# A streaming-encoder layer on one core: who stores the operands of the first pair, in what order its loads, splits and sums stand, and where the fourth row tile lives

## The reference

```
h    = rmsnorm(x) * norm_g                       # 1024 x 2048
proj = h @ w_in                                  # 2048 x 5120, cut into nine parts
       A: u, v, gate (512 each)   spatial gating: u * (W_s @ layernorm(gelu(v)) + b_s)
       B: q (1024), k, v (256 each), gate (1024)   sliding-window attention with sinks and a bias
       C: input, gate (512 each)  trailing means over 2, 4, 8, 16 positions, a linear map, a scale
mix  = concat(A, B, C), each times silu(its gate)
x    = x + mix @ w_out                           # 2048 x 2048
out  = rmsnorm(x) * final_g
```

## Time and profile before

| what | value |
|---|---|
| median of 3 runs (lowest, highest) | 1207.43 us (1206.47, 1209.11) |
| the profiled execution: its time, its span | 1209.07 us, 1207.3 us |
| TensorE / VectorE / ScalarE busy, share of the span | 97% / 72% / 41% |
| mean TensorE clock granted | 0.991 of full |
| DMA moved | 361.27 MB, 299 GB/s |

### The profile page before, as it was taken

How to read it: one execution, slowest core, us unless ns; L and a number is a source line. 1 busy time by engine, 2 the same in 40 slices (tenths; PEclk the granted TensorE clock), 3 DMA queues, 4 the chain that set the end, 5 groups by cost and what they waited for, 6 DMA issues and landing times.

```text
span 1207.3 us, 15660 instructions
## 1 busy us (share of the span) xinstructions
PE 1176.0 (97%) x5862; PEld 956.6 (79%) x5862; DVE 872.0 (72%) x1150; ACT 493.4 (41%) x867; POOL 39.7 (3%) x80
## 2 busy tenths in 40 slices
PE   9989899999999999999999999999999999999995
PEld 7768788888888888888888877778877788888884
DVE  5589857586976776788677797988788366564675
ACT  5465564523544333355433362423344213323135
POOL 0012110000000000000000000000000000000000
PEclk9999899999999999999999999999999999999998
DMA  9989899877865565995566586699999689956878
GB/s 341 412 326 361 348 422 369 249 270 247 340 236 181 201 229 213 326 374 192 196 238 254 210 322 253 239 325 364 419 411 408 256 309 401 376 212 233 297 278 330
DMA packets 105772, 361.27 MB, mean 299 GB/s; under 512 B 10945, under 2 KB 18145, under 8 KB 94817
## 3 DMA queue, kind: packets, MB, share of 16 engines
q1 hardware_dynamic: 99936, 339.30, 76.1%
q0 software_dynamic: 5760, 20.97, 4.3%
HBM read 288.67 MB, written 71.57 MB: 298 GB/s over the span
## 4 chain that ended last, share of the span: by engine, by line
PE 74%; DVE 12%; DMA 8%; SPq 2%; issue 2%; ACT 1%; ACTq 0%; DVEq 0%
PE n_bank L1800 23%; PE n_bank L1802 22%; PE n_bank L1801 22%; DMA x_parts<-s_ring 3%; DVE w_lo L1255 2%; PE e_bank L1951 2%; DVE w_b L1380 2%; PE t_bank L1979 2%; PE t_bank L1962 1%; DMA w_b<-w_b_dram 1%; DMA m_parts<-tg 1%; DMA m_parts<-stage 1%; DVE s_ring L1264 1%; DMA rows<-x_dram 1%; SPq L529 1%
## 5 line engine op out<-in xcount | busy, mean ns | idle before, releaser
L924 ACT ACTIVATE w_hi<-w_b 128x1024 fp32r<-128x1024 f32 (+1 forms) x200 | 197.4, 1033 | 435.7 <-PE n_bank L1802 387.2
L1800 PE MATMUL n_bank<-s_ring,w_hi 128*128 128x512 f32 x896 | 356.8, 398 | 0.0
L1802 PE MATMUL n_bank<-s_ring,w_lo 128*128 128x512 f32 x896 | 349.0, 390 | 0.0
L1801 PE MATMUL n_bank<-s_ring,w_hi 128*128 128x512 f32 x896 | 348.9, 389 | 0.0
L1255 DVE TENSOR_TENSOR w_lo<-w_b,w_hi 128x1024 fp32r<-128x1024 f32 (+1 forms) x200 | 231.6, 1198 | 113.6 <-ACT w_hi L924 113.3
L1800 PE MATMUL n_bank<-w_hi,s_ring 128*128 128x512 f32 x672 | 266.2, 396 | 16.0 <-DVE w_lo L1255 5.8
L1801 PE MATMUL n_bank<-w_lo,s_ring 128*128 128x512 f32 x672 | 263.8, 393 | 0.0
L1802 PE MATMUL n_bank<-w_hi,s_ring 128*128 128x512 f32 x672 | 263.8, 392 | 0.0
L1800 PEld LDWEIGHTS n_bank<-s_ring,w_hi 128*128 128x128 f32 x896 | 168.1, 188 | 39.3 <-issue 2.2
L1802 PEld LDWEIGHTS n_bank<-s_ring,w_lo 128*128 128x128 f32 x896 | 168.2, 188 | 35.7
L1801 PEld LDWEIGHTS n_bank<-s_ring,w_hi 128*128 128x128 f32 x896 | 168.3, 188 | 35.3 <-issue 1.9
(11 more groups left out here) (211 smaller groups left out, 949.1 us busy)
## 6 DMA issues: line engine op xcount, KB each, us to landing
s_ring<-x_parts SPq DMA_DIRECT2D x224, 512.0 KB, 6.0
w_b<-w_b_dram SPq DMA_DIRECT2D x74, 1024.0 KB, 10.6
s_ring<-m_parts SPq DMA_DIRECT2D x112, 512.0 KB, 6.2
x_parts<-s_ring POOLq DMA_DIRECT2D x40, 512.0 KB, 10.2
m_parts<-stage SPq DMA_DIRECT2D x18, 512.0 KB, 8.3
x_parts<-s_ring SPq DMA_DIRECT2D x16, 512.0 KB, 15.1
rows<-x_dram SPq DMA_DIRECT2D x8, 1024.0 KB, 12.3
residual<-x_dram SPq DMA_DIRECT2D x6, 1024.0 KB, 9.2
```

The source lines that it names most:

```text
L924: sc.activation(w_hi[:, J % 2, part], w_source(J)[:, part], ACT.Copy).then_inc(hi_done, 1)
L1800: pe.matmul(psum_out, stat[0], mov[0], start=first, stop=False)
L1801: pe.matmul(psum_out, stat[0], mov[1], start=False, stop=False)
L1802: return pe.matmul(psum_out, stat[1], mov[0], start=False, stop=last)
```

## The change

It has these parts:

1. SyncE stores the operand tiles of periods 0 and 1 alone, GpSimd those of 2 to 13 (SAVED_EARLY 4 to 2). At n = 2 and n = 3 SyncE now waits until the four stores of that period have landed (`saves_done`), ahead of the a22 quads.
2. At the start each a11 tile is loaded ahead of the weight piece of its number, and in step 1 the operand is split ahead of the weights.
3. A11 + A12: the banks of A12 aren't copied by ScalarE any more; VectorE adds them straight to A11 in `add_chain` (in its steps 3 and 4), and `sum_y11` in step 6 is gone. `bank_free` of step 4 waits for that add.
4. In steps 3 and 4 the splits of weights and operands of the next step alternate differently on ScalarE and VectorE: first operand tile, weights, other operand tiles.
5. Row tile 3 has home 1 and is loaded at n = 9 (before: home 0, n = 8), tile 4 home 2 at n = 10 (before home 1, n = 9), tiles 5 and 6 homes 3 and 4, tile 7 home 3 again. The first add of S1 waits for three squared tiles, not four. The squares stand at the end of ScalarE's step; root, row factors and layer constants of the first half are one step later.

```diff
@@ -86,7 +86,7 @@
-ADDS = ({Q_A11: 0, Q_A12: 0, Q_S3: 0, Q_S2: 1, Q_S1: 2, Q_S4: 1, Q_A22: 1},) + tuple(
+ADDS = ({Q_A11: 0, Q_A12: 1, Q_S3: 0, Q_S2: 1, Q_S1: 2, Q_S4: 1, Q_A22: 1},) + tuple(
     {Q_A12: 1 if p >= PAIR_O or not early(p) else 0, Q_A11: 1 if early(p) else 0, Q_S2: 1, Q_S1: 2,
@@ -101,7 +101,7 @@
 def first_copies(p, st):
-    return ST * sum(1 for b in range(p) if early(b) and b < PAIR_O) + st + 1
+    return ST * sum(1 for b in range(PAIR_TA, p) if early(b) and b < PAIR_O) + st + 1
@@ -136,9 +136,9 @@
 ROW_TILES = HALVES * ST
-ROWS_LOADED = {5: 0, 6: 1, 7: 2, 8: 3, 9: 4, 11: 5, 13: 6, 15: 7}
-AT_ROOT = (10, 17)
-AT_ROWS = (12, 19)
+ROWS_LOADED = {5: 0, 6: 1, 7: 2, 9: 3, 10: 4, 11: 5, 13: 6, 15: 7}
+AT_ROOT = (11, 17)
+AT_ROWS = (13, 19)
 AT_KV = (13, 18)
@@ -146,7 +146,15 @@
 AT_SGU = ((17, 18), (20, 21))
-SAVED_EARLY = 4
+SAVED_EARLY = 2
+
+ROW_HOME = (0, 0, 0, 1, 2, 3, 4, 3)
+
+
+def row_loads(t):
+
+    return sum(1 for i in ROW_HOME[:t + 1] if i == ROW_HOME[t])
+
@@ -322,7 +330,7 @@
         row_buffers = [place(f"rows{i}", [P, D], offset=home) for i, home in enumerate(row_homes)]
-        row_tile = [row_buffers[max(t - ST + 1, 0)] for t in range(ROW_TILES)]
+        row_tile = [row_buffers[i] for i in ROW_HOME]
         kv = (y11[PAIR_F], y21[PAIR_F])
@@ -460,7 +468,7 @@
         w_loaded = [[sem(f"w_loaded{b}{c}") for c in range(2)] for b in range(3)]
-        w_summed, y11_summed, y21_summed = sem("w_summed"), sem("y11_summed"), sem("y21_summed")
+        w_summed, y21_summed = sem("w_summed"), sem("y21_summed")
         first_copied, p1_copied, u_copied = sem("first_copied"), sem("p1_copied"), sem("u_copied")
@@ -529,17 +537,24 @@
+            def saves_done(n):
+
+                for k in range(4):
+                    sp.wait_ge(f_saved_late[first_slot(n, k)[1]], 16 * ((n - SAVED_EARLY) // 2 + 1))
+
...
                     sp.wait_ge(f_lo_done, 20)
-                elif t < ST:
+                elif t < 3:
                     sp.wait_ge(rows_squared, t)
-                elif t < ST + 2:
+                elif t < 5:
                     sp.wait_ge(f_lo_done, 40)
+                elif t < 7:
+                    sp.wait_ge(s4_made, KB)
                 else:
-                    sp.wait_ge(s4_made, KB)
-                sp.dma_start(row_tile[t][:], x[P * t:P * t + P, :]).then_inc(rows_loaded[max(t - ST + 1, 0)], 16)
+                    sp.wait_ge(rows_squared, 6)
+                sp.dma_start(row_tile[t][:], x[P * t:P * t + P, :]).then_inc(rows_loaded[ROW_HOME[t]], 16)
@@ -551,7 +566,7 @@
             def load_layer_constants():
-                sp.wait_ge(rows_squared, 5)
+                sp.wait_ge(rows_squared, 4)
                 for dst, src in ((ln_g_sb[:], rows(ln_g, 512)), (ln_b_sb[:], rows(ln_b, 512)),
@@ -764,8 +779,8 @@
             for r in range(1, KB):
+                load_a11(r)
                 load_first(r // 4, r % 4)
-                load_a11(r)
             second, third = BUFS[0][1:]
@@ -778,6 +793,8 @@
                     save_early(n + 1)
+                if n in (2, 3):
+                    saves_done(n)
                 if n < 2:
@@ -790,7 +807,7 @@
                     save_table()
-                if n == 10:
+                if n == 11:
                     load_layer_constants()
@@ -962,7 +979,7 @@
-                sc.wait_ge(rows_loaded[max(t - ST + 1, 0)], 16 * (t + 1) if t < ST else 16)
+                sc.wait_ge(rows_loaded[ROW_HOME[t]], 16 * row_loads(t))
                 sc.activation(row_tile[t][:], row_tile[t][:], ACT.Square, accum_out=ssq_x[:, t:t + 1]
@@ -982,12 +999,12 @@
                 sc.wait_ge(f_lo_done, 4 * STEPS)
-                sc.wait_ge(rows_squared, ST + 2)
+                sc.wait_ge(rows_squared, 5)
                 if half == 1:
...
                     if half == 0:
-                        sc.wait_ge(y11_summed, st + 1)
+                        sc.wait_ge(y_added, added(PAIR_F, Q_A12, st))
                     else:
@@ -1113,7 +1130,7 @@
                     q = ORDERS[pp][jj // 2]
-                    if q == Q_A12 and early(pp) and pp < PAIR_O:
+                    if q == Q_A12 and early(pp) and PAIR_F < pp < PAIR_O:
                         copy_first(pp, sts)
@@ -1170,19 +1187,18 @@
                     for k in range(4):
+                        first_hi(1, k)
                         split_hi(1, (k,))
-                        first_hi(1, k)
                 elif J + 1 < TOTAL and J not in SUM_S3:
...
                 if 0 < J < STEPS - 1:
-                    for k in range(4):
+                    first_hi(J + 1, 0)
+                    if J in SUM_S3:
+                        split_hi(J + 1)
+                    for k in range(1, 4):
                         first_hi(J + 1, k)
-                if J in SUM_S3:
-                    split_hi(J + 1)
                 for r in SCALE_A22.get(J, ()):
                     scale_a22(r)
-                if J - 1 in ROWS_LOADED:
-                    square_rows(ROWS_LOADED[J - 1])
                 if J == AT_TABLE + 1:
@@ -1217,6 +1233,8 @@
                         job(kind, i)
+                if J - 1 in ROWS_LOADED:
+                    square_rows(ROWS_LOADED[J - 1])
                 if j == 2 * EARLY.index(Q_S2) + 1 and early(p) and p > PAIR_F:
@@ -1423,7 +1441,7 @@
                 if p == PAIR_F:
-                    ve.wait_ge(rows_squared, ST)
+                    ve.wait_ge(rows_squared, 3)
                 elif p == PAIR_TA:
@@ -1453,7 +1471,10 @@
                     wait_chain(ve, bank_done, group_done, n, st)
-                    if q == Q_A12:
+                    if q == Q_A12 and p == PAIR_F:
+                        ve.wait_ge(p1_copied, p1_copies(p, st))
+                        add(y11[p], st, y12[p])
+                    elif q == Q_A12:
                         if early(p):
@@ -1492,13 +1513,6 @@
-            def sum_y11(st):
-
-                ve.wait_ge(first_copied, first_copies(PAIR_F, st))
-                ve.wait_ge(p1_copied, p1_copies(PAIR_F, st))
-                ve.tensor_tensor(y11[PAIR_F][:, st, :], y11[PAIR_F][:, st, :], y12[PAIR_F][:, st, :], ALU.add
-                                 ).then_inc(y11_summed, 1)
-
@@ -1672,8 +1686,8 @@
                     for k in range(4):
+                        first_lo(1, k)
                         split_lo(1, (k,))
-                        first_lo(1, k)
                 if 0 < n < STEPS - 1:
@@ -1686,17 +1700,15 @@
                         first_lo(n + 1, 0)
+                        split_lo(J + 1, (0,))
                         first_lo(n + 1, 1)
-                        split_lo(J + 1)
+                        split_lo(J + 1, (1,))
                         first_lo(n + 1, 2)
...
                             first_lo(n + 1, k)
-                if n == 6:
-                    for st in range(ST):
-                        sum_y11(st)
                 if n == 8:
@@ -1834,7 +1846,7 @@
                 q = ORDERS[p][at]
-                if q == Q_A12 and early(p) and p < PAIR_O:
+                if q == Q_A12 and early(p) and PAIR_F < p < PAIR_O:
                     pe.wait_ge(first_copied, first_copies(p, st))
```

## The result

| | before | after |
|---|---|---|
| median of 7 runs (lowest to highest), us | 1207.43 (1206.47 to 1209.11) | 1211.76 (1209.50 to 1212.65) |
| profiled execution, its span | 1209.07, 1207.3 | 1211.76, 1210.0 |

The ratio after to before is 1.0030, 95% interval 1.0018 to 1.0042: slower by a little more than the 0.2% that can be told from no change. The range ended at 1210.7, so the result lies outside it, on the side of the second rival.

A forecast was written before the change was run, and what follows sets the result against it. TensorE, busy 97%, was the bound, so only its gaps could give time. 10.4 us lost at step 4 against gains at steps 5 and 10 left 2.1 us less: 1205.3 us median, range 1199 to 1210.7.

The forecast's parts named there:

- the second rival: Step 14: DMA backlog delays period 12's stores and the loads they release; 3.3 us more, 1210.7; chance 0.18.
- a third of the bytes: Before step 4: GpSimd's stores take a third of DMA bytes, SyncE's 7.34 MB take 26.5 us, B22's first half lands at 54.9.
- the first rival: Step 4: only period 2's stores pass B22, landing 50.8; step 4 starts at 59.8; 6.8 us less, 1200.6; chance 0.26.
- 9.0 us from B22's landing to step 4: Head of step 4: weight sum, splits, remaining tiles and the bank-freeing add take 9.0 us, so it starts at 64.5.
- The 4.54 us of its wait: Head of step 5: TensorE's wait, put down to SyncE's period 3 stores, goes: 4.54 us, plus 1.7 of clock.
- the sum: Steps 4 to 11: losses and gains added up to 2.1 us less, step 11 at 142.9, 1207.0 profiled, 1205.3 median.
- 10.4 us lost against some 6 won: Steps 4 and 5: 10.4 us lost at step 4; 4.54 of gap and 1.7 of clock won back at step 5.
- 6.5 forecast: Step 10: the wait for row tile 3 goes, worth 3.73 us between two steps and 2.75 of clock.
- its wait of 3.2 us: Step 14: the last load lands 2.4 us later while the need is 2.1 earlier, so TensorE waits 3.2.
- its 2.2 of clock: Step 14: the clock drop after the wait costs another 2.2 us.
- The third rival: Step 10: the first S1 add waits for VectorE's or the DMA's backlog; 4.4 us more, 1211.8; chance 0.04.
- a margin of 1.3 us at step 14's last load: Step 14: the last load landed at 179.3 before the change, 1.3 us ahead of TensorE's need.

The follow-up runs named there:

- e8b_stores_tiles: The kernel before with parts 1 and 5, without parts 2 to 4; 1208.53 us, ratio 1.0001.
- e1_stores_back: The changed kernel with part 1 undone: SyncE stores periods 0 to 3 again, without its two waits; 1204.37 us, ratio 0.9975.
- e13_back_later: e1_stores_back with row tile 5 loaded at n = 13 and tiles 5 to 7 behind the coming step's slot loads; 1199.93 us, ratio 0.9939.
- e2_tiles_only: The kernel before with part 5 alone; 1207.47 us, ratio 1.0006.
- e3: The changed kernel with row tiles 4 and 5 loaded and squared in their first 64 columns only, 2 MB less read; 1206.63 us, ratio 0.9997.
- e12: The changed kernel with row tile 5 loaded at n = 13 and tiles 5 to 7 behind the coming step's slot loads; 1207.59 us, ratio 1.0000.
- e14: e2_tiles_only with row tile 5 loaded at n = 13 and tiles 5 to 7 behind the coming step's slot loads; 1204.29 us, ratio 0.9981.

## Why the prediction was wrong

**Right, part 1.** B22's first half was to land at 55.5 and landed at 56.3; period 2's stores at 36 to 43 (measured 33.0 to 41.0), period 3's at 50 to 57 (47.3 to 56.3). The mechanism stands: undone, step 4 is back at 54.4. What I chose badly was the rate at which GpSimd's stores go past. I took a third of the bytes, from a stretch of 16 us. The DMA view of the changed kernel from 30 to 33 us, while its period 2 stores were under way (queue, packets, MB, share of the engines' time):

```profile
q1 hardware_dynamic: 192, 0.62, 51.2%
q0 software_dynamic: 169, 0.63, 51.0%
```

Half each, to the per cent (and 51.4 to 52.5 from 44.5 to 47.3). The third of the earlier trace rows was a mean over a stretch in which GpSimd's queue was empty part of the time. This is what the Trainium skill ("DMA: Bandwidth & Descriptors", section on queues, rings and completion order) says, turns between the queues that have work; the trace agrees. By it all eight stores are past B22, landing 55.9, 0.4 from what was measured, and the first rival, stores that slip past at less cost, had nothing left to stand on: 0.26 was too much for it. As a mean the third holds in the changed kernel too: from 28.0 to 56.3, the whole way of B22's first half, GpSimd's queue moved 4.19 of 11.60 MB, 36%, and all eight stores were past it all the same.

**Right, parts 3 and 4.** 9.0 us from B22's landing to step 4; measured 65.2 - 56.3 = 8.9. The wait ended on a VectorE add, as named. Not seen: that before's order, kept, would have needed only 5.0 us (issued 28.0, landed 27.7 later, step 4 at 60.7 in e8b_stores_tiles). So the late weight turned parts that win 4.4 us into ones that cost 3.8 at step 4.

**Right in number, wrong in cause, step 5.** The 4.54 us of its wait were won as forecast, but the sum gives part 1 the credit. With SyncE's stores back the wait is gone (e1_stores_back) or 0.74 us (e13_back_later): parts 2 to 4 do it alone, by the traces part 4. So part 1 was costed as a trade, 10.4 us lost against some 6 won, where beside the other parts it had next to nothing left to win. Step 3 lost 1.4 us to period 1's later stores, not 3, and that was hidden under step 4's wait as forecast.

**Right, part 5 up to step 11.** No wait at step 10; VectorE kept up; in e2_tiles_only it was worth 6.4 us there, against 6.5 forecast. Step 5 at 78.5 (forecast 77.6), step 11 at 143.8 (142.9): 0.9 late, of which 0.7 came in with step 4, no more than executions of the same code differ there. Between steps 11 and 14 0.4 of it was made up.

**The step that failed** was "From step 11 on I see nothing that changes by more than 0.2". In its place step 14 grew from 11.7 to 16.4 us: 4.7 us more. That is nearly all of the 4.8 us by which the profiled execution (1211.76) missed the 1207.0 that the sum gave for it. In the terms of the second rival: its wait of 3.2 us was 3.4; its 2.2 of clock wasn't paid in the changed kernel (1.00 from 148 to 190), though it was in e1_stores_back (0.92); another 1.3 of step 14 is spread over its starts. It gave 1210.7 for the median and so 1212.4 for the profiled execution; both were 1211.76. The third rival's 1211.8 is the measured number by chance: the wait at step 10 that it rests on didn't come.

So the case was on the list, with its sign (a wait of PE for s_ring at step 14), and had the wrong chance. What spoke for it were a DMA share of 1.02 on both sides of one idle stretch, and a margin of 1.3 us at step 14's last load. Two errors kept it at 0.18. First, I costed the later loads of tiles 3 and 4 at nothing because nothing waits for them. What counts is what is queued behind them: tile 4 moved to 141.5, and the constants from 140 to 147, into the one stretch that gave the DMA time to catch up. Every experiment with part 5's times of loading shows the longer step 14, with or without part 1 (e2 17.4, e8b 17.1, after 16.4 us), and most of it goes when the tiles' bytes go (e3, 12.1) or tile 5 goes behind (e12, e13, e14, 13.1 to 13.5). Second, I put its mechanism into the stores of period 12 alone. They do release the loads, as I had it, but they landed in 15.8 us instead of 17.0, the last 1.1 later than before and not 2.4. The larger part is behind the release: step 14's loads took 13.2 instead of 7.6, with tile 5, the constants and two weight loads issued ahead of them in SyncE's own queue.

The chance of 0.26 for slower came mostly from this rival. That 1.6 us of the miss against the median are the difference between one execution and the median was in the text, but as an offset that would repeat; it didn't.

## What to carry over

Where the DMA is full on both sides of a short idle stretch, that stretch is the reserve of all that is loaded next: a load moved into it is costed by what is queued behind it, not by who waits for it. A store moved to an idle engine's queue landed sooner here by taking half of the DMA from the main queue while both had work, so first ask what stands in that queue in the same microseconds. A wait can have two cures, here other stores or another order of the splits; priced one by one against the kernel before, the second looks as good as the first, and together one of them is only a cost. And a gain at one wait is only kept if the next load's margin is larger than the gain; here 6.4 us won at step 10 left 1.1 at step 15 until one 1 MB load was put behind the loads that step 14 needs, and 5.1 after that (e2_tiles_only, e14_before_later).

## What the runs showed of the hardware

With both DMA queues busy, each got 51% of the engines' time in a stretch of 3 us of the changed kernel. The stores of 512 KB by GpSimd landed in 7.2 to 11.9 us, while SyncE's of period 1, issued ahead of them into its own full queue, took 19.2 to 22.6.

A full DMA share isn't one rate: from 97 to 137 us the engines were 1.00 busy in the changed kernel at 373 GB/s, 1.02 busy before at 416. The runs don't show why.

The granted clock fell to 1.2 GHz after the wait of 11.96 us at step 4 (0.50 of full until 70.0: 11 matmuls 0.43 us apart instead of 0.23), but three waits of 0.7 to 1.4 us inside step 14 left it at 1.00 in the changed kernel and brought the mean of the stretch to 0.92 in e1_stores_back, where the waits were no longer (0.56, 1.36, 0.58; 0.70 of full from 174.4 to 184.0). So step 14 lasted 16.4 us with 3.4 us of waits in one, and 18.3 with 2.5 in the other.
